# A conditioning product in four column strips, spread over three stages

## The reference

```
mod = silu(c) @ w_mod[l] + b_mod[l]            # (9 rows, 1024) @ (1024, 6144)
sh1, sc1, g1, sh2, sc2, g2 = split(mod, 6)
y, state = mixer(x * (1 + sc1) + sh1)          # layer 0: retention; layer 1: sparse attention
x = layer_norm(ALPHA * x + g1 * y)
f = grouped_moe(x * (1 + sc2) + sh2)           # router, top 2 of 16 experts
x = layer_norm(ALPHA * x + g2 * f)
```

## Time and profile before

| | |
|---|---|
| median of three runs | 2306.9 us |
| span of the profiled execution, first to last instruction | 2300.9 us |
| the profiled execution's own whole time | not listed; the median is 6.0 us above the span |
| PE busy | 1980.4 us (86%) |
| DVE, ACT, POOL busy | 1083.0, 755.0, 240.0 us |
| DMA | 412.17 MB, mean 179 GB/s |
| granted TensorE clock, mean | 0.912 of 2.4 GHz |

### The profile page before, as it was taken

One profiled execution on the slowest core, in us unless ns is written; L12 is line 12 of the kernel. 1 busy time (PEld: TensorE's weight loads), 2 busy tenths in 40 slices (PEclk: granted clock), 3 DMA queues, 4 the chain that ended last, 5 costly groups with the idle time before them and its releaser, 6 DMA issues.

```text
span 2300.9 us, 20268 instructions
## 1 busy us (share of the span) xinstructions
PE 1980.4 (86%) x6641; PEld 1054.0 (46%) x6641; DVE 1083.0 (47%) x1673; ACT 755.0 (33%) x969; POOL 240.0 (10%) x237
## 2 busy tenths in 40 slices
PE   7999999999899999979999659996668981999990
PEld 1243323443333335247787523443343551877770
DVE  0220143220352017158988581116752173989886
ACT  0011021110211001058887411113442021887861
POOL 0000010000000000362221110000000003212201
PEclk9999999999999997989999879995776875999995
DMA  9822154121172122989999831112002233999983
GB/s 331 315 108 73 46 193 144 46 73 65 63 256 85 72 73 106 318 290 393 392 393 391 291 111 45 53 34 61 1 0 74 84 138 101 341 393 392 393 306 121
DMA packets 196224, 412.17 MB, mean 179 GB/s; under 512 B 15646, under 2 KB 19806, under 8 KB 196127
## 3 DMA queue, kind: packets, MB, share of 16 engines
q1 hardware_dynamic: 168962, 322.26, 39.1%
q0 software_dynamic: 21008, 71.10, 8.1%
q10 hardware_dynamic: 6184, 17.93, 2.3%
HBM read 363.36 MB, written 47.90 MB: 179 GB/s over the span
## 4 chain that ended last, share of the span: by engine, by line
PE 70%; DVE 10%; DMA 6%; issue 4%; ACT 4%; DVEq 3%; POOL 1%; ACTq 1%; POOLq 0%; SPq 0%
PE bank L564 38%; PE bank L818 17%; PE bank L557 3%; DMA RING<-in_w_gate 3%; PE bank L754 3%; ACT WH L1229 2%; PE bank L739 1%; PE bank L908 1%; PE bank L728 1%; DMA mod_d<-BC 1%; DVEq L2071 1%; DVE WL L1926 1%; POOL slot_d L1505 1%; DVE m L2068 1%; PE bank L724 1%
## 5 line engine op out<-in xcount | busy, mean ns | idle before, releaser
L564 PE MATMUL bank<-RING,HT 128*128 128x512 f32 (+3 forms) x1600 | 683.0, 583 | 11.9 <-ACT HT L1074 9.3
L1926 DVE TENSOR_TENSOR WL<-RING,WH 128x2048 fp32r<-128x2048 f32 x192 | 438.0, 2301 | 136.9 <-ACT WH L1229 135.1
L564 PEld LDWEIGHTS bank<-RING,HT 128*128 128x128 f32 (+1 forms) x1600 | 263.4, 172 | 384.4 <-issue 374.2
L1229 ACT ACTIVATE WH<-RING 128x2048 fp32r<-128x2048 f32 x192 | 364.8, 1915 | 117.1 <-PE bank L818 92.1
L557 PE MATMUL bank<-cst,M 128*128 128x128 f32 (+3 forms) x721 | 112.5, 286 | 124.6 <-DVE M L1597 40.1
L818 PE MATMUL bank<-WH,HGH 128*128 128x512 f32 x512 | 204.9, 400 | 6.4 <-DVE HGL L1937 6.4
L818 PE MATMUL bank<-WH,HGL 128*128 128x512 f32 x512 | 201.4, 393 | 0.0
L818 PE MATMUL bank<-WL,HGH 128*128 128x512 f32 x512 | 201.1, 393 | 0.0
L557 PEld LDWEIGHTS bank<-cst,M 128*128 128x128 f32 (+3 forms) x721 | 90.4, 153 | 182.5 <-issue 77.4
L564 PE MATMUL bank<-RING,CT 128*9 128x512 f32 x384 | 168.3, 600 | 0.3 <-DVE CT L1658 0.3
L564 PE MATMUL bank<-RING,M 128*128 128x512 f32 (+1 forms) x320 | 138.6, 593 | 0.3 <-ACT M L1183 0.3
(11 more groups left out here) (263 smaller groups left out, 2028.3 us busy)
## 6 DMA issues: line engine op xcount, KB each, us to landing
RING<-in_w_gate SPq DMA_DIRECT2D x64, 1024.0 KB, 11.0
RING<-in_w_up SPq DMA_DIRECT2D x64, 1024.0 KB, 12.3
RING<-in_w_down SPq DMA_DIRECT2D x64, 1024.0 KB, 11.5
RING<-in_w_mod SPq DMA_DIRECT2D x24, 2048.0 KB, 9.3
RING<-in_w_in_ret SPq DMA_DIRECT2D x12, 2048.0 KB, 8.2
RING<-in_state_ret SPq DMA_DIRECT2D x16, 1024.0 KB, 7.2
out_ret_sample<-RING POOLq DMA_DIRECT2D x16, 1024.0 KB, 6.8
RING<-in_w_in_dsa SPq DMA_DIRECT2D x5, 2048.0 KB, 7.8
```

The costliest lines, as they stand in the source:

```text
L564: last = pe.matmul(out, lhs[:, k, :], w[:, k, :], start=start and k == 0, stop=stop and k == K - 1)
L1229: act.activation(WH[:, u % SPLIT, :, :], raw(u % RAW), ACT.Copy).then_inc(S("hi_rdy"), 1)
L1926: TT(WL[:, u % SPLIT, :, :], raw(u % RAW), WH[:, u % SPLIT, :, :].bitcast(F32), ALU.subtract)\
```

## The change

The number of weight bytes, blocks and results stays the same. What changes:

- A block's 8 matmuls go to four strips of 32 columns: matmul k multiplies `CT[:, k]`, padded with zeros to 32 columns, into partitions 32j to 32j + 31 of the bank, j = k mod 4, two matmuls to a strip (`mod_mm`). ACT copies the 128 x 512 bank to SBUF (`mod_part`). One more matmul with a 0/1 matrix `gsum` (128 x 9) adds the four strips (`mod_sum`). DVE (first eight of layer 0 after the first four, and those four) or ACT (`mod_row`) takes the 9 x 512 result.
- Blocks 0 to 3 come first. Blocks 4 to 11 are laid singly ahead of the products of retention: k, v, v and the second g of the first pair of heads, q, k, v, v of the second; each is summed two products later. POOL stores each.
- Blocks 12 to 17 stay in routing, two before the ranks, four after; ACT does all six evictions ahead of `high`; POOL adds the biases after the gathers and stores all six at once.
- Blocks 18 to 23 come after the experts. SP loads three of them when the last expert weights are split, the rest follow in the stream; the wait for the combination's tiles goes. ACT evicts blocks 18 to 20 before it gates the first tile and 21 to 23 before tiles 1 to 3. POOL adds the bias to all six in one instruction, 1 to the scale in another, and stores once.
- Four constant loads move from ACT's queue to POOL's. ACT waits for blocks 4 to 11 to be stored before the `YT` copies of the second pair of heads, and for the last store before its second eviction of the attention projection, because their places in SBUF are used again.

```diff
         stream, state_uses = [], [0] * 3
-        for n in range(12):
-            stream.append((("mod", 0, n), [("mod_mm", n + 1)]))
+        mods = iter(range(24))
+        def mod_blocks(count):
+            for _ in range(count):
+                g = next(mods)
+                stream.append((("mod", g), [("mod_mm", g + 1)]))
+        mod_blocks(MOD_FIRST)
...
             ret = lambda i: [("ret_mm", (6 * hp + i + 1) * TILES)]
-            stream += [(("q", hp), ret(0)), (("k", hp), ret(1)), (("v", hp, 0), ret(2)), (("v", hp, 1), ret(3))]
+            for i, key in enumerate((("q", hp), ("k", hp), ("v", hp, 0), ("v", hp, 1))):
+                mod_blocks(1 if hp or i else 0)
+                stream.append((key, ret(i)))
...
                 stream.append((("state", hp, b2), [("os_mm", 4 * n), (f"state_st{s}", 32 * state_uses[s])]))
-            stream += [(("g", hp, 0), ret(4)), (("g", hp, 1), ret(5))]
+            stream.append((("g", hp, 0), ret(4)))
+            mod_blocks(1 - hp)
+            stream.append((("g", hp, 1), ret(5)))
...
             stream.append((("out0", n, 1), [("out_mm0", TILES * (n + 1))]))
-        for n in range(12):
-            stream.append((("mod", 1, n), [("mod_mm", 12 + n + 1)]))
+        mod_blocks(MOD_ROUTE - MOD_RET)
         N_FIRST = len(stream)
+        mod_blocks(24 - MOD_ROUTE)
...
                     sp.wait_ge(S("lo_rdy"), (first + last) * len(UNITS) + (len(UNITS) + UNIT0))
-                    load(stream[N_FIRST][0])
-                    sp.wait_ge(S("cmb0"), TILES - 1)
...
+                    loads(stream[N_FIRST:N_FIRST + 3])
...
             moe_loads(0)
-            loads(stream[N_FIRST + 1:])
+            loads(stream[N_FIRST + 3:])
...
             pe.wait_ge(S("c_t"), 1)
-            for n in range(12):
-                wait_slot(pe, ("mod", 0, n))
-                if n >= 2:
-                    pe.wait_ge(S("mod_ev"), n - 1)
-                rhs_mm(bank[n % 2][0:R, :], CT, slot(("mod", 0, n)), "mod_mm")
-            def mod1(part):
-                for n in part:
-                    wait_slot(pe, ("mod", 1, n))
-                    if n == 0:
-                        pe.wait_ge(S("out_ev0"), 2 * TILES)
-                    if n >= 4:
-                        pe.wait_ge(S("mod_ev"), 12 + n - 3)
-                    rhs_mm(bank[2 + n % 4][0:DEC + 1, :], CT, slot(("mod", 1, n)), "mod_mm")
+            def mod_mm(g, out):
+                wait_slot(pe, ("mod", g))
+                w = slot(("mod", g))
+                for kk in range(KD // 4):
+                    for j in range(4):
+                        k = 4 * kk + j
+                        last = pe.matmul(out[32 * j:32 * j + 32, :], CT[:, k, :], w[:, k, :], start=kk == 0,
+                                         stop=kk == KD // 4 - 1)
+                last.then_inc(S("mod_mm"), 1)
+            def mod_sum(g, out, parts):
+                pe.wait_ge(S("mod_mp"), g + 1)
+                pe.matmul(out[0:DEC + 1, :], C("gsum"), parts[g % 2], start=True, stop=True).then_inc(S("mod_red"), 1)
+            def mod_group(part, begin, end, out, total, parts):
+                for g in part:
+                    if g >= begin + 2:
+                        pe.wait_ge(S("mod_mp"), g - 1)
+                    mod_mm(g, out[g % 2])
+                    if g > begin:
+                        if g >= begin + 3:
+                            pe.wait_ge(S("mod_ev"), g - 2)
+                        mod_sum(g - 1, total[(g - 1) % 2], parts)
+                    if g == end - 1:
+                        pe.wait_ge(S("mod_ev"), g - 1)
+                        mod_sum(g, total[g % 2], parts)
+            mod_group(range(MOD_FIRST), 0, MOD_FIRST, bank[0:2], bank[4:6], MP0)
+            mods = iter(range(MOD_FIRST, 24))
+            def mod_between():
+                g = next(mods)
+                pe.wait_ge(S("mod_ev"), g - 1)
+                mod_mm(g, bank[4 + g % 2])
+                return g
+            def mod_between_sum(g):
+                mod_sum(g, bank[6 + g % 2], MP0)
...
                     qk += 1
+                between = None
                 for i in range(2 * TILES):
+                    if i % TILES == 0 and (hp or i):
+                        between = mod_between()
...
                         turn_qk()
+                    if i % TILES == 1 and (hp or i > 1):
+                        mod_between_sum(between)
+                between = mod_between()
...
                 for i in range(1, 2 * TILES):
+                    if i == TILES:
+                        between = mod_between()
                     ret_product(("v", hp, i // TILES), i % TILES)
+                    if i % TILES == 1:
+                        mod_between_sum(between)
...
                 pe.wait_ge(S("ret_ev"), item)
+                pe.wait_ge(S("mod_ev"), between + 1)
...
                 if l == 0:
-                    mod1(range(0, 2))
+                    pe.wait_ge(S("out_ev0"), 2 * TILES)
+                    mod_group(range(MOD_RET, MOD_RET + 2), MOD_RET, MOD_ROUTE, bank[2:4], bank[4:6], MP1)
...
                 pair(first + last, True)
+                if l == 0:
+                    mod_group(range(MOD_ROUTE, 24), MOD_ROUTE, 24, bank[0:2], bank[2:4], MP2)
...
             act.activation(CSIL[:, :], CROW[:, :], ACT.Silu).then_inc(S("c_silu"), 1)
-            act.wait_ge(S("mod_ev"), 4)
-            act.dma_start(mod_d[0][:, 0:2 * D], MODV[:, 0:2 * D]).then_inc(S("mod_st0"), 16)
+            def mod_part(g, src, parts):
+                act.wait_ge(S("mod_mm"), g + 1)
+                if g >= 2:
+                    act.wait_ge(S("mod_red"), g - 1)
+                act.activation(parts[g % 2], src, ACT.Copy).then_inc(S("mod_mp"), 1)
+            def mod_row(g, dst, src):
+                act.wait_ge(S("mod_red"), g + 1)
+                act.activation(dst, src[0:DEC + 1, :], ACT.Copy).then_inc(S("mod_ev"), 1)
+            for g in range(MOD_FIRST):
+                mod_part(g, bank[g % 2][:, :], MP0)
+            act.wait_ge(S("mod_ev"), MOD_FIRST)
+            act.dma_start(mod_d[0][:, 0:MOD_FIRST * NB], MODV[:, :]).then_inc(S("mod_st0"), 16)
             scale_shift(0)
-            act.wait_ge(S("mod_ev"), 12)
-            act.dma_start(mod_d[0][:, 2 * D:], MODV[:, 2 * D:]).then_inc(S("mod_st0"), 16)
-            def mod1(n):
-                act.wait_ge(S("mod_mm"), 12 + n + 1)
-                if n >= 6:
-                    act.wait_ge(S("mod_st1"), 16 * (n - 5))
-                act.activation(MS1[n % 6], bank[2 + n % 4][0:DEC + 1, :], ACT.Copy).then_inc(S("mod_ev"), 1)
+            mods = iter(range(MOD_FIRST, MOD_RET))
+            def mod_between():
+                g = next(mods)
+                mod_part(g, bank[4 + g % 2][:, :], MP0)
...
                 turned(0, t)
-            act.wait_ge(S("mod_st0"), 32)
...
                 if l == 0:
-                    for n in range(10):
-                        mod1(n)
+                    for g in range(MOD_RET, MOD_ROUTE):
+                        mod_part(g, bank[2 + g % 2][:, :], MP1)
+                        if g > MOD_RET:
+                            mod_row(g - 1, MS1[g - 1 - MOD_RET], bank[4 + (g - 1) % 2])
+                    mod_row(MOD_ROUTE - 1, MS1[MOD_ROUTE - 1 - MOD_RET], bank[4 + (MOD_ROUTE - 1) % 2])
...
                 if l == 0:
-                    act.wait_ge(S("mod_st1"), 16 * 12)
+                    act.wait_ge(S("mod_st1"), MOD_ST[1])
...
                 if l == 0:
+                    act.dma_start(BM2, A["b_mod"][1:2, (MOD_ROUTE - 12) * NB:].to_broadcast([DEC + 1, (24 - MOD_ROUTE) * NB]))\
+                        .then_inc(S("bmod_in"), 16)
...
                     scale_shift(m + 1)
+                def mod_late(g):
+                    mod_part(g, bank[g % 2][:, :], MP2)
+                    if g > MOD_ROUTE:
+                        mod_last(g - 1)
+                def mod_last(g):
+                    mod_row(g, MS2[:, (g - MOD_ROUTE) * NB:(g - MOD_ROUTE + 1) * NB], bank[2 + g % 2])
+                if l == 0:
+                    for g in range(MOD_ROUTE, MOD_ROUTE + 3):
+                        mod_late(g)
                 for s in range(TILES + 3):
+                    if l == 0 and 1 <= s <= 3:
+                        mod_late(MOD_ROUTE + 2 + s)
+                    if l == 0 and s == 4:
+                        mod_last(23)
...
                 act.wait_ge(S("d_mm"), i + 1)
+                if i == 1:
+                    act.wait_ge(S("mod_st1"), MOD_ST[2])
...
             pool.dma_start(slot_d.rearrange("(p i) o -> p (i o)", p=P), zero_i[:, :]).then_inc(S("slot_zero"), 16)
+            def bias(g):
+                pool.dma_start(bias1[:, g % 4, :], A["b_mod"][g // 12:g // 12 + 1, g % 12 * NB:(g % 12 + 1) * NB]
+                               .to_broadcast([DEC + 1, NB])).then_inc(S(f"bm_in{g % 4}"), 16)
+            def mod_store(g):
+                pool.wait_ge(S("mod_ev"), g + 1)
+                if g > MOD_FIRST:
```

(57 more changed lines are left out.)

117 lines of the change are left out of this document (73 added, 44 removed).

## The result

The changed kernel takes **2275.8 us** in the median of four runs (2269.8 to 2277.3), the kernel before 2307.2 beside it: ratio 0.9856, 95% interval 0.9839 to 0.9872. That is 31.4 us faster; 2261 was forecast, with a range of 2241 to 2298. The profiled execution has a span of 2275.6 us, 25.3 less than before. So the forecast's change of -46 is to be held against -25, and its 6.0 us between span and median against 1.7 (this execution took 2277.34 us as a whole).

The account below looks back on a forecast made before the run. PE was taken as busy nearly throughout the first two stages and layer 0's routing; ACT's waits for stores held routing's end. -40 + 22 - 39 + 11 = -46; 2300.9 - 46 + 6.0 = 2261 us, range 2241 to 2298.

Parts of the forecast that it names:

- Strips: A block's eight matmuls in four column strips: all four run together, 1.7 us of PE; 6.9 if they queue.
- rival 1: Half the gain from strips: a strip's two instructions hold back the next strip, 3.4 us a block; 2281 us; chance 0.12.
- rival 2: Strips queue on PE one after the other: retention costs 63 instead of 22, 2316 us in all; chance 0.10.
- First stage: Start to retention's first product: DMA becomes the limit, block 3 lands at about 38, stage ends at 71 instead of 111.6: -40.
- The lower clock: First stage: PE idles between loads, so 0.86 us an instruction; block 3's product takes 3.4 us.
- Retention: PE-bound stage with eight blocks laid in between, 2.8 us of PE each: +22 (20 to 24; 63 if strips queue).
- Routing: Router to first expert product: start read from POOL's gather chain, 967 against 1006.3: -39 (-34 to -43).
- Combining: After layer 0's experts, six blocks: DVE starts at 1331 instead of 1321.33, stage ends +11 (+4 to +23).
- 12.0 MB at 0.38 a microsecond: Combining: bytes from 1294 to the first gathers take 31 us; block 20 lands between 1319 and 1327, 1324 taken.
- Ahead of ACT's second eviction: Combining: POOL's bias additions for six blocks, 10 us, end at about 1375, before ACT's eviction that waits for them.
- Rival 3: Combining: the six loads go ahead of the gathers altogether, DVE starts at 1344: +23, 2273 us; chance 0.10.
- From span to median: Median of the runs shown, 2306.9, is 6.0 above the span of 2300.9; 6.0 added to the forecast span.

## Why the prediction was right, and where its sizes were off

- **Strips: right.** Four run together; rivals 1 and 2 fall, and one strip costs what was reckoned for it (7.05 us). The Trainium skill, "TensorE: Matmul & The Clock Gate", What overlaps and what doesn't, has matmuls start and end in program order. By it, if the two instructions of a matmul stand next to each other, as rival 1 had it, 16 instructions would have taken eight times 0.43 at the least, 3.4 us. They took 1.92: either they don't stand so or the order doesn't hold back another strip, and the trace doesn't tell which.
- **First stage: right**, -39.5 against -40, by errors that cancel, which is luck. The store was issued 1 us sooner (43.9 instead of 45) and took 4.6 to the next issue instead of 6.9; the scale and shift loads took 9.9 from their first issue, 8.7 from their last, instead of 6. The lower clock was taken from combining as the stage where PE idles most; by the earlier trace rows that is layer 1's routing (2.7 of 55.1 us busy, 0.50), and the term came out near all the same (3.29 for 3.4).
- **Retention: +28.5 against +22.** The term of 2.8 us a block measures 2.9 to 3.2 (24.7 for eight); 1.4 is the first two tiles, which start at the lower clock after PE's wait (0.50 of 2.4 GHz to 75 us), and the rest the two steps over the samples, 1.2 each, where PE has half the clock for 10 us instead of 7.
- **Routing: right**, -36.5 against -39. It ends with the gather. Six blocks have six places, so no eviction waits for a store; the few stores were worth nothing there, but 7 us in the experts, and one strip instead of four costs routing 3.4. Twelve blocks with twelve places were not tried.
- **Combining: +21.1 against +11; the step that failed.** Block 20 landed 29.6 us behind the experts, not 23, and ACT's gating stood behind it. "12.0 MB at 0.38 a microsecond" was too little at too high a rate: the DMA moved 12.9 MB at 352 GB/s, some 0.6 of them of block 21, whose load was issued at 1257.45. That is 2.3 us for the bytes and 2.7 for the rate; the rest of the 6.6 is that 1324 was taken where 12.0 MB at 0.38 from 1294 on give 1325.6. "Ahead of ACT's second eviction" asked only who waits for POOL's result; nobody does, but while POOL added, DVE stood for 6.3 us at one step and 0.7 at the next. The Trainium skill, "SBUF — State Buffer", Who interferes with whom, says that a DVE instruction with two inputs in SBUF and a GpSimd instruction that reads SBUF exclude each other, and the one that issues second waits for all of the first; the trace agrees (7.52 for 1.23, ending 1.1 behind POOL's), and that rule belonged in the forecast. POOL's second instruction agrees less: it lasts 4.49 us, and the DVE step that began 1.1 us after it lost only 0.7. Rival 3 had the size, +23, but not the cause: the gathers did not queue behind all six loads, they came 5 us late.
- **From span to median: 6.0 was wrong** as the gap between the two, though harmless in the sum, which sets the change against the median. An execution is 1.7 us longer than its span (2277.34 and 2275.6; up to 2.9 in other runs). The other 4.3, an estimate from these, was that the profiled execution of the kernel before was one of its quicker ones (2302.0 to 2316.9 in 17 runs). The changed kernel's was the slowest of its four, so the medians changed by 31.4 and the spans by 25.3. By the spans the forecast is off by 20.7 us, of which 10.1 are combining; by the medians, by 15.

## What to carry to other kernels

Work that fills gaps belongs where all its engines and the DMA wait: the same block cost 5.7 us in a stage bound by loads (45.6 for eight), 3.1 where PE is bound, 3.5 in combining (21.1 for six, of which 12 were ACT's order and POOL's additions), and nothing in the attention. Before an off-path instruction is priced at nothing, ask whom it excludes while it runs, not only who waits for its result. And where an engine's queue mixes early work with work that waits for a late load, put the early work first.

## What the runs showed of the hardware

- Matmuls into four 32-partition strips of one bank, each with its own 128 rows, run fully together: 1.92 us for 16 instructions of 512 columns, 7.05 in one strip.
- POOL's addition of two SBUF operands (9x3072) stopped DVE's step with two SBUF operands until its end and 1.1 us more, in every run that kept it in combining (7.50 to 7.68 us); with the bias on PE the same step took 1.23.
- 120 more PE instructions in the attention went with a granted clock of 0.74 instead of 0.65 to 0.69 of 2.4 GHz, and the stage was no longer for them.
